# A decoder block in fp32: the down projection as seven half products, with sums of weights made by transfers

## The reference, cut to what matters

```python
def conv_gated_mlp(x, w_up, conv_w, w_down):
    h = causal_dwconv(x @ w_up, conv_w)
    gt, val = jnp.split(h, 2, axis=-1)
    return (jax.nn.silu(gt) * val) @ w_down
...
    for l in range(DEPTH):
        h = rms_norm(x, norm_mix_pre[l])
        (gq, gk, ...) = jnp.split(h @ w_in[l], split_idx, axis=-1)
...
        mix = jnp.concatenate([o_a, o_b, o_c], axis=-1) @ w_out[l]
        x = x + rms_norm(mix, norm_mix_post[l])
        h = rms_norm(x, norm_ffn_pre[l])
        x = x + rms_norm(conv_gated_mlp(h, ffn_w_up[l], ffn_conv_w[l], ffn_w_down[l]), norm_ffn_post[l])
```

## Time and profile before

| | us |
|---|---|
| median of 3 executions (1061.56 to 1064.03) | 1063.03 |
| the profiled execution | 1061.33 |
| its span, first to last instruction | 1059.6 |
| PE, VectorE, ScalarE, GpSimd busy | 1023.5, 814.0, 634.9, 500.8 |

### The profile page before, as it was taken

One profiled execution on the slowest core, in us unless ns is written; L12 is line 12 of the kernel. 1 busy time (PEld: TensorE's weight loads), 2 busy tenths in 40 slices (PEclk: granted clock), 3 DMA queues, 4 the chain that ended last, 5 costly groups with the idle time before them and its releaser, 6 DMA issues.

```text
span 1059.6 us, 19099 instructions
## 1 busy us (share of the span) xinstructions
PE 1023.5 (97%) x7136; PEld 831.5 (78%) x7136; DVE 814.0 (77%) x1140; ACT 634.9 (60%) x1201; POOL 500.8 (47%) x653
## 2 busy tenths in 40 slices
PE   5999999998999999999999999999999998999997
PEld 4878878986777778777688787888887786888885
DVE  5798895756668886877586598899999999646755
ACT  7544423347777777777865455666666667446443
POOL 2457423726454565551410278788788886000000
PEclk9999999999999999999999999999999999999999
DMA  8245311352122112012263612234433335955962
GB/s 274 71 128 171 115 52 27 75 121 58 41 60 60 36 44 60 19 29 61 90 222 126 199 41 80 80 123 129 130 126 122 121 110 210 371 170 182 331 240 80
DMA packets 159523, 126.78 MB, mean 120 GB/s; under 512 B 63908, under 2 KB 137928, under 8 KB 159432
## 3 DMA queue, kind: packets, MB, share of 16 engines
q1 hardware_dynamic: 157992, 120.32, 37.8%
q10 hardware_dynamic: 1440, 5.24, 1.2%
HBM read 99.79 MB, written 25.71 MB: 118 GB/s over the span
## 4 chain that ended last, share of the span: by engine, by line
PE 57%; DVE 9%; issue 4%; POOL 4%; ACT 3%; DMA 0%; DVEq 0%; ACTq 0%; POOLq 0%
PE psum L2490 14%; PE psum L2278 9%; PE psum L1786 5%; PE psum L1735 5%; PE psum L1719 4%; POOL slab_q L2102 4%; PE psum L1551 4%; PE psum L1901 3%; PE psum L1702 3%; PE psum L2284 2%; DVE arena L2186 2%; DVE arena L2180 1%; DVE arena L2225 1%; DVE psum L2232 1%; PE psum L1632 1%
## 5 line engine op out<-in xcount | busy, mean ns | idle before, releaser
L2102 POOL TENSOR_TENSOR slab_q<-arena,slab_p 128x512 fp32r<-128x512 f32 x127 | 208.2, 1668 | 45.5 <-ACT slab_p L2095 45.4
L2490 PE MATMUL psum<-dn_p,ap_p 128*128 128x512 f32 x352 | 110.3, 393 | 2.7 <-DVE arena L2186 1.4
L2490 PE MATMUL psum<-dn_q,ap_q 128*128 128x512 f32 x352 | 109.8, 391 | 0.0
L2278 PE MATMUL psum<-t_p,slab_p 128*128 128x512 f32 x272 | 106.3, 391 | 1.3 <-ACT arena L2159 0.8
L2278 PE MATMUL psum<-t_q,slab_q 128*128 128x512 f32 x272 | 105.9, 389 | 0.0
L2095 ACT ACTIVATE slab_p<-arena 128x512 fp32r<-128x512 f32 x127 | 78.2, 628 | 38.7 <-PE psum L2278 13.8
L2316 DVE TENSOR_TENSOR dn_q<-arena,dn_p 128x1024 fp32r<-128x1024 f32 x41 | 50.2, 1224 | 56.3 <-ACT dn_p L2306 56.3
L1431 DVE CUSTOM_DVE_ANT_0 psum<-psum,arena 128x640 f32<-128x640 f32 (+7 forms) x96 | 67.8, 717 | 29.8 <-PE psum L1702 29.2
L2306 ACT ACTIVATE dn_p<-arena 128x1024 fp32r<-128x1024 f32 x44 | 46.6, 1059 | 70.0 <-PE psum L2490 65.6
L3066 PE MATMUL psum<-h_p,cm_p 128*128 128x512 f32 (+1 forms) x288 | 86.4, 372 | 0.6 <-DVE arena L2973 0.6
L3066 PE MATMUL psum<-h_q,cm_q 128*128 128x512 f32 (+1 forms) x288 | 85.8, 371 | 0.0
(11 more groups left out here) (321 smaller groups left out, 2632.3 us busy)
## 6 DMA issues: line engine op xcount, KB each, us to landing
arena<-in_ffn_w_up SPq DMA_DIRECT2D x44, 512.0 KB, 5.2
arena<-in_ffn_w_down SPq DMA_DIRECT2D x44, 512.0 KB, 4.0
arena<-in_w_in SPq DMA_DIRECT2D x20, 512.0 KB, 3.9
act_mid<-arena SPq DMA_DIRECT2D x18, 512.0 KB, 2.6
arena<-act_mid SPq DMA_DIRECT2D x36, 256.0 KB, 5.0
arena<-in_x SPq DMA_DIRECT2D x16, 512.0 KB, 4.8
qkv_mid<-arena ACTq DMA_DIRECT2D x9, 512.0 KB
arena<-qkv_mid SPq DMA_DIRECT2D x8, 576.0 KB, 4.6
```

The source lines that it names most:

```text
L2102: pool.tensor_tensor(slab_q[n % RING], part_source(i, j), slab_p[n % RING], ALU.subtract).then_inc(late("up_lo")[0], 1)
L2278: ins = pe.matmul(mult_ps(i, j), w[:, k], x[:, k], start=k == 0 and x is x_p[i] and i in (1, 2, 5), stop=True, skip_group_check=True)
L2490: ins = pe.matmul(dn_ps[t % HT][:, n * 512:(n + 1) * 512], x[:, tok], w[:, n * 512:(n + 1) * 512], start=first and x is ap_p[s], stop=True ...
```

## The change

The down product is cut in halves of the tokens, of the 2816 inner rows and of the 1024 columns. In place of eight half products it computes seven, of sums of halves (numbers 1 to 7, in the order 1, 2, 6, 5, 7, 3, 4), each of 11 steps of 128 inner rows, 4 token tiles and 512 columns: 77 steps of 8 matmuls (`DN_STEPS`). Products 1, 6, 7 and 4 add up in four PSUM banks (`acc_x`), 2, 5 and 3 use the other four (`acc_y`); ACT copies three intermediate results out (`copied_out`), VectorE adds three (`joined`).

The sums of activations (`row_sum`: S3, S2, Z1, S4, eleven of each) are made on VectorE, 128 x 512 each, behind the operand splits of steps 8 to 50. Four sums of weights (`w_sums`, 1408 x 512 each) are made in HBM by DMAs that GpSimd issues (`down_sums`): two copies behind GpSimd's splits of unit 5 of the input projection and two additions behind those of unit 10; then in the up stage a copy behind l1.11, an addition behind l1.13, a copy behind l1.16 and an addition behind l1.18, each after a wait for the one before.

Weight blocks are half as wide, on eight buffers (`W_RING`); operand blocks have four (`A_RING`). The first ten q parts of weights are made by GpSimd, the others by VectorE. Six steps in place of three begin inside the up stage's order. Spilled activations are reloaded in half rows, the first eight during the last block of the up stage. The residual rows go into freed activation buffers. Squares of three quarters of the result are taken while later products run; GpSimd multiplies these quarters by the norm's weights. All eight stores lie at the end.

The core of the diff, added lines only:

```diff
+HK = NF // 2
+DN_MULTS = (1, 2, 6, 5, 7, 3, 4)
+DN_STEPS = [(i, k) for i in DN_MULTS for k in range(HK)]
+DN = len(DN_STEPS)
+W_RING, A_RING = 8, 4
+UP_TAIL = 6
+DN_POOL_LO = list(range(10))
+DN_DVE_LO = [n for n in range(DN) if n not in DN_POOL_LO]
...
+    "e_add": ("c_ss", 8 + 3 * len(SEVEN)),
+    "d_s": ("g_ss", 8 + 4 * len(SEVEN)),
+    "d_y": ("q_hi", 12),
...
+        x1r = lambda t: act_f[t]
+        left_d, right_d = slice(0, HALF_D), slice(HALF_D, D)
+        c11, c12 = [[y_dn[:, t, c] for t in range(HT)] for c in (left_d, right_d)]
+        c21, c22 = [[y_dn[:, HT + t, c] for t in range(HT)] for c in (left_d, right_d)]
+        s2 = [R.view(w, [HALF_D]) for w in (18432, 18944, 19456, 19968, 27648, 28160)] + c21
+        acc_x, acc_y = [[psum[:, HT * h + t] for t in range(HT)] for h in range(2)]
+        acc_of = lambda i: acc_x if i in (1, 6, 7, 4) else acc_y
...
+        def down_sums(pool, t):
+
+            w11, w12, w21, w22 = [a["ffn_w_down"][0, h * HK * P:(h + 1) * HK * P, c * HALF_D:(c + 1) * HALF_D] for h in range(2) for c in range(2)]
+            one, two, three, four = [w_sums[n] for n in range(4)]
+            if t == 5:
+                pool.dma_start(one, w11).then_inc(sem("wt"), 16)
+                pool.dma_start(three, w12).then_inc(sem("wt"), 16)
+            elif t == 8:
+                pool.wait_ge(sem("wt"), 32)
+                pool.dma_start(one, w12, accum_op=ALU.add).then_inc(sem("wt"), 16)
+                pool.dma_start(three, w22, accum_op=ALU.add).then_inc(sem("wt"), 16)
+            elif t == 11:
+                pool.wait_ge(sem("wt"), 64)
+                pool.dma_start(two, one).then_inc(sem("wt"), 16)
+            elif t == 13:
+                pool.wait_ge(sem("wt"), 80)
+                pool.dma_start(two, w22, accum_op=ALU.add).then_inc(sem("wt"), 16)
+            elif t == 16:
+                pool.wait_ge(sem("wt"), 96)
+                pool.dma_start(four, two).then_inc(sem("wt"), 16)
+            elif t == 18:
+                pool.wait_ge(sem("wt"), 112)
+                pool.dma_start(four, w21, accum_op=ALU.add).then_inc(sem("wt"), 16)
+
...
+            def act_begin(part):
+                mult_done(sp, 5 + part, SEVEN[-1])
+                for j in (HK - 2, HK - 1):
+                    spilled(sp, j)
+                for n in range(4 * part, 4 * part + 4):
+                    act_reload(sp, n)
...
+            def part_lo(i, j):
+                split_mult_lo(pool, i, j)
+                if i == 1 and j > 8:
+                    down_sums(pool, j)
...
+        WSUM_OF = {5: 0, 6: 1, 7: 2, 4: 3}
+
+        def down_source(n):
+
+            i, k = DN_STEPS[n]
+            if i in WSUM_OF:
+                return w_sums[WSUM_OF[i], k * P:(k + 1) * P, :]
+            row = (k if i == 1 else k + HK) * P
+            return a["ffn_w_down"][0, row:row + P, right_d if i == 3 else left_d]
+
...
+                down_landed(sp, n - 4)
+            if n >= W_RING:
+                dn_ready(sp, n - W_RING)
+            sp.dma_start(dn_st[n % W_RING], down_source(n)).then_inc(late(f"dn_st{n % 4}")[0], 16)
...
+        RELOAD_AT = sorted([(-1, 0, k) for k in range(CLASSIC, HK)] + [(13 + k, 0, k + HK) for k in range(HK - 1)]
+                           + [(12 + 2 * k, 1, x) for k in range(HK) for x in (k, k + HK) if CLASSIC <= x < NF - 1])
...
+        for k in range(HK):
+            SUMS_AT[8 + 2 * k].append(("S3", k))
+            SUMS_AT[9 + 2 * k].append(("S2", k))
+            SUMS_AT[30 + k].append(("Z1", k))
+            SUMS_AT[40 + k if k else 28].append(("S4", k))
...
+            if n >= A_RING:
+                act.wait_ge(*late("dn_mm", n - A_RING + 1))
...
+            for n in range(UP_TAIL, DN):
+                if n == DN_STEPS.index((6, 0)):
+                    sp.wait_ge(sem("wt"), 128)
+                down_load(sp, n)
+                while reload < len(RELOADS) and RELOAD_AT[reload][0] <= n:
+                    act_reload(sp, reload)
+                    reload += 1
+                if n == 10:
                     sp.dma_start(gpost_ffn, a["norm_ffn_post"][0].partition_broadcast(P)).then_inc(sem("gpost2_in"), 16)
+                if n == 64:
+                    sp.wait_ge(*late("ap_lo", DN_STEPS.index((7, NT - 1)) + 1))
                     x1_loads(0)
...
+                if n == 72:
                     x1_loads(1)
...
+            for n in range(UP_TAIL, DN):
+                for i, at_ in ((1, 15), (6, 37), (5, 48)):
+                    if at_ <= n < at_ + 2:
+                        copied_out(i, 2 * (n - at_))
+                        copied_out(i, 2 * (n - at_) + 1)
+                if 54 <= n < 58:
+                    act.wait_ge(*late("e_add", n - 54 + 1))
+                    squares(n - 54, c11[n - 54], n - 54)
+                if 62 <= n < 66:
+                    act.wait_ge(*late("e_add", HT + n - 62 + 1))
+                    squares(2 * HT + n - 62, c22[n - 62], HT + n - 62)
+                if 71 <= n < 75:
+                    act.wait_ge(*late("e_add", 2 * HT + n - 71 + 1))
+                    squares(HT + n - 71, c12[n - 71], 2 * HT + n - 71)
+                dn_split_hi(act, n)
+                act_split_hi(act, n)
...
+            act.wait_ge(*late("f_b", 1))
+            act.activation(wrs[:, 0:HT], wrs[:, 2 * HT:3 * HT], ACT.Ln, bias=eps_w, scale=1.0 / D).then_inc(late("f_ln")[0], 1)
+            act.wait_ge(*late("f_ln", 1))
+            act.activation(wrs[:, 0:HT], wrs[:, 0:HT], ACT.Exp, scale=-0.5).then_inc(late("f_rs")[0], 1)
+            act.wait_ge(*late("f_rs", 1))
+            for t in (2, 3):
+                act.wait_ge(*late("d_y", 2 * HT + t + 1))
+                act.activation(y_dn[:, t], y_dn[:, t], ACT.Copy, scale=wrs[:, t:t + 1]).then_inc(late("e_cp")[0], 1)
...
+            def row_sum(name, k):
+                if name == "S3":
+                    act_landed(v, 0, k)
+                    act_landed(v, 1, k)
+                    out, x, y, op = quarter(0, k), quarter(0, k), quarter(1, k), ALU.subtract
+                elif name == "S2":
+                    row_sum_done(v, "S3", k)
+                    act_landed(v, 1, k + HK)
+                    if k == 0:
+                        v.wait_ge(*late("up_mm", 2 * CLASSIC + PRODUCTS))
+                    if k >= len(s2):
+                        row_sum_done(v, "S4", k - len(s2))
+                    out, x, y, op = s2[k % len(s2)], quarter(0, k), quarter(1, k + HK), ALU.add
+                elif name == "Z1":
+                    row_sum_done(v, "S3", k)
+                    out, x, y, op = quarter(1, k), quarter(1, k + HK), quarter(1, k), ALU.subtract
                 else:
...
+            for n in range(UP_TAIL, DN):
+                for i, at_ in ((2, 26), (7, 59), (3, 69)):
+                    if at_ <= n < at_ + 2:
+                        joined(i, 2 * (n - at_))
+                        joined(i, 2 * (n - at_) + 1)
+                if n in DN_DVE_LO:
+                    dn_split_lo(v, n)
+                act_split_lo(v, n)
+                for x in SUMS_AT[n]:
+                    row_sum(*x)
...
+            for t in range(2):
+                half_one(t)
...
+                pool.wait_ge(*late("e_cp", 3 * HT + t - 1))
+                pool.wait_ge(*late(f"x1r{t}", 16))
+                pool.tensor_tensor(y_dn[:, t], y_dn[:, t], x1r(t), ALU.add).then_inc(late("fin_p")[0], 1)
 
         def down_pe(pe):
...
+            def pair(n, t, first):
+                i, k = DN_STEPS[n]
+                tok = slice(t * P, (t + 1) * P)
+                for x, w in ((ap_p[n % A_RING], dn_p[n % W_RING]), (ap_q[n % A_RING], dn_q[n % W_RING])):
+                    ins = pe.matmul(acc_of(i)[t], x[:, tok], w, start=first and x is ap_p[n % A_RING], stop=True, skip_group_check=True)
                 return ins
 
...
+            own_k = 4
+            for n in range(DN - own_k):
+                i, k = DN_STEPS[n]
+                ready(n)
+                for t in range(HT):
+                    if k == 0:
+                        free(i, t)
+                    ins = pair(n, t, k == 0 and i in (1, 2, 5))
+                ins.then_inc(late("dn_mm")[0], 1)
+            for t in range(HT):
+                for n in range(DN - own_k, DN):
+                    if t == 0:
+                        ready(n)
+                    ins = pair(n, t, False)
+                ins.then_inc(late("dn_t")[0], 1)
 
         def piece_load(sp, n):
             kind, c = PIECES[n]
@@ -2727,6 +2866,8 @@
             for i in range(U_KC):
...
+                if i in (5, 10):
+                    down_sums(pool, {5: 5, 10: 8}[i])
```

More of the change, by code:

```diff
@@ new lines, in build, with row_sum_done, act_split_hi @@
+        D_SUMS = sum(SUMS_AT.values(), [])
+        def row_sum_done(eng, name, k):
+            eng.wait_ge(*late("d_s", D_SUMS.index((name, k)) + 1))
+        def act_split_hi(act, n):
+            i, k = DN_STEPS[n]
+            if i == 1:
+                act_landed(act, 0, k)
```

(33 more changed lines are left out.)

367 lines of the change are left out of this document (152 added, 215 removed), and 6 rows, old and new, of the table UP_ORDER.

## The result

The changed kernel takes 1108.98 us (four runs, 1106.68 to 1116.83) where the kernel before, on the same chip, takes 1063.45; the ratio of the means is 1.0444 (95% interval 1.0391 to 1.0497). It is slower by 4.4%. The prediction was 1047.9 us, in a range that ended at 1062.5. The profiled execution has a span of 1107.2 us, 47.6 more than before.

What follows compares the result with a forecast made beforehand. The prediction took PE to bound the down stage. From the median of 1063.03 us, -20.0 - 2.6 + 1 + 0.5 + 2 + 4 = -15.1 gave 1047.9 us, range 1041 to 1062.5.

Steps and rivals of the forecast that it cites:

- Weight sums: Eight transfers in input and up stages: +4 us (0; at most 35) for GpSimd's issues, 0 for the data moved.
- Issues: GpSimd held while issuing transfers: 2 us per up-stage copy, 4 per addition, +4 in all; input stage 0.
- Rival 4: Slower: GpSimd held while each transfer moves, up stage 35 us, input stage up to 14.7; 1078.9 or 1093.6; chance 0.12.
- Fewer products: Down stage: 616 matmuls replace 704, 88 fewer at 0.2275 us each, -20.0 us if PE stays fed.
- Start of the stage: Beginning of the down stage: a PE gap of 2.5 us in place of 5.1, -2.6 us (0 to -4).
- 1043.9: Predicted time in us if the issues of the transfers are short and their +4 is 0.
- Row sums and tail: Down stage: VectorE row sums in steps 8 to 50, +1 us (0 to +4); work behind PE's end, +2 (+1 to +4).
- Reloads: Down stage: weight loads and activation reloads, 7.9 MB due in 20 us on nearly full queues; +0.5 us (0 to +4).

Runs made afterwards that it cites:

- no_transfers: The changed kernel without its eight transfers of weight sums, with plain w_down blocks loaded in products 5, 6, 7 and 4; 1059.66 us.
- bare_down: no_transfers with GpSimd's last six operations (four multiplications, two residual additions) and the 44 VectorE row sums left out; 1047.54 us.
- vector_tail: no_transfers with GpSimd's two residual additions and the two ACT scalings ahead of them made two VectorE operations; 1056.18 us.

## Why the prediction was wrong

It was 61.1 us too low (1108.98 - 1047.9).

**The step that failed is in "Weight sums": "The data itself: the queues are 0.40 busy there, the w_up loads land in 5.2 us and are needed a block of 13 us later; 0."** In its place stand 49.3 us (predicted with the issues: 4), so 45.3 of the error. Three things were wrong in it.
- A mean share of 0.40 says that the queues have room for 11.5 MB in 200 us. It doesn't say that a load issued 3 us behind 2.9 MB lands in 5.2 us.
- The lead is not a block of 13 us. The order of the up stage has h1 of the next block ahead of this block's last split on GpSimd (l7), so the first use comes 7.1 us after the issue (783.40 to 790.52), 2 us after a normal landing.
- I had worked out 7.2 and 14.4 us as the time in which a copy and an addition move, and used them only for GpSimd's being held. They had about the size of the delay of two of the loads (12.4 - 5.1 = 7.3 and 18.5 - 5.1 = 13.4), on other engines: DMA to ACT to PE. That 14.4 fits so well is luck: the additions landed after 21.1 and 22.9 us, the loads were issued 2.8 us behind them, and the one beside the first addition was some 16 us late.

Of the up stage's 39.2 us, 31.4 are PE's waits. Of the rest much is clock: it is 0.87 from 780 to 804 us and 0.85 from 804 to 830 (below, columns as in the earlier trace rows), where no_transfers has 1.00 in both.

```profile
804.00:830.00 26.00, 22.23 (x90) 18.26 (x91) 22.60 (x21) 16.78 (x26) 18.45 (x13) 0.85 0.35 105
```

The input stage, put at 0 with an upper bound of 14.7, took 10.5, by the same mechanism and not by late GpSimd splits for their own sake.

**Issues.** Mis-sized: the issues took 0.55 to 0.59 us for a copy in the up stage and 1.46 to 1.49 for an addition, against 2 and 4. The rule that the prediction cited from the Trainium skill ("DMA: Bandwidth & Descriptors", section Anatomy of one DMA) holds in the main: 1408 rows cost GpSimd 0.9 us more than a contiguous copy did, and PE nothing. Rival 4, the only one on the slow side, had the wrong place: GpSimd was never held for more than 2.2 us.

**Fewer products**: right, 616 matmuls at 0.2275 us. Where nothing is late, in bare_down, the stage is 148.4 = 140.1 + 8.3.

**Start of the stage**: wrong by more than the whole term, -2.6. The 5.1 us of gaps in the kernel before were not all at its start. PE's waits there, 885 to 905 us:

```profile
PE psum L2490 <- DVE arena L2186: 1.4, 2, 1.0
PE psum L2490 <- DVE ap_q L2355: 0.9, 1, 0.9
```

By starts of matmuls 3.3 us are lost there; 0.6 more are lost near 1040, and about 1 is spread over the stage. No wait was over 1.03 us, and the clock stayed at 1.00 from 890 to 905. After, there is one wait of 4.1 us, not 2.5: ACT's table load ended 13.2 us behind the stage's first matmul in the changed kernel (952.5 - 939.3) and 9.9 before, so 3.3 later in place of 1.2 to 2.4. In bare_down the clock falls to its lower level behind this wait: the window 905 to 910 has 0.50, and twelve matmuls 0.43 us apart cost 2.4 us. By starts 7.1 us are lost, so -2.6 was +3.8. That bare_down lies only 3.6 above 1043.9 is because that sum also holds +1 for row sums, +0.5 for reloads and +0.5 for GpSimd in the tail, which bare_down doesn't pay or which came out as 0.

**Row sums and tail**: +1 and +2 were expected, of which 1.5 was VectorE's own tail; left out together, row sums and GpSimd's last work give 12.1 us (1059.66 - 1047.54) in place of 1.5. The +1 held where I looked, in steps 8 to 50. The error was to cost each against PE alone. That VectorE's cover "is used up at steps 26 to 28 and nothing is left" was in the text, and from it follows that any later loss of VectorE reaches PE; the loss came from about step 54 on, where GpSimd multiplies by the norm's weights and later adds residuals. I had costed GpSimd beside VectorE's last additions only. By "SBUF — State Buffer", section Who interferes with whom, of the Trainium skill the two hold the ports in turn; the rows of 2.84 and 2.82 beside 2.78 show it, and it had to be applied to each GpSimd operation of the stage. VectorE's tail without GpSimd was right: 8.4 us from the last matmul's start in bare_down against 6.9, +1.5.

**Reloads**: right. They held ACT for 2.2 us in all and PE not at all, with a DMA share of 0.96 for 20 us (960 to 980).

In sum the terms missed by 45.3 (transfers), 10.6 (row sums and GpSimd), 6.4 (start) and -0.5 (reloads), 61.8 in all. The error is 61.1; most of the difference is that the kernel before took 1062.39 beside the later runs, 0.6 less than the median that the prediction counted from.

Open: why the first packet of a load issued behind a transfer started only 4 to 5 us after its issue (783.4 to 787.6 beside the first addition).

## What to carry to other kernels

A background transfer is costed by what is issued beside it: take the next load on any queue, count on it to land only when the transfer has (here 1.5 to 4.1 us passed between the transfer's landing and the first use; a load with far fewer packets than the transfer was not tried), and compare that with the first use as the engines' order has it, not with a block's length. Put the transfer where no load and no exchange through memory is due within its 11 to 23 us, even if that is hundreds of us early. And where an engine works at its limit, add up what slows it when it runs beside it over the whole rest of the stage, since without a lead every loss arrives at PE, and behind a gap the lower clock comes on top.

## What the runs showed of the hardware

- 2.9 MB within HBM: a copy landed after 11.1 us in quiet queues, an accumulating addition after 18.9 to 19.5, a plain copy of the same rows beside loads after 14.2. By 403 GB/s it would have been 7.2 and 14.4.
- While GpSimd's transfer (q0) and SP's load (q1) both had work, they were served one packet each in turn, with packets of 0.5 KB against 2 KB (739 to 737) and 0.5 KB against 4 KB (153 to 154).
- An issue can take long beside a transfer: SP's spill took 8.87 us to issue in place of 0.34, with a load and an addition under way. The time that a GpSimd issue takes (0.5 to 2.2 us) says nothing of what the transfer costs.
- Two additions moved from GpSimd to the busier VectorE did not make VectorE later: its last two splits fell from 2.84 and 2.82 to 0.68 us each (vector_tail).
